# Closing PSUM banks one by one over two rows ahead of a norm, and moving weight splits between engines

## The reference

```
first block, two layers:   hs = hs + rms_norm(mixer(rms_norm(hs)))     mixer: gated delta net, then mLSTM
                           hs = hs + rms_norm(conv_ffn(rms_norm(hs)))
second block, two layers:  x = layer_norm(ALPHA * x + mixer(x))        mixer: conv + window attention, then GLA + MLA
                           x = layer_norm(ALPHA * x + swiglu(x))
```

## Time and profile before

| | |
|---|---|
| three runs | 1445.07, 1447.41, 1447.57 us; median 1447.41 us |
| profiled execution | span 1443.1 us from its first to its last instruction; no other time is given for it. The median lies 4.3 us above the span |
| busy share | PE 99%, PEld 95%, DVE 70%, ACT 54%, POOL 20% |
| mean granted clock of TensorE | 0.999 |
| weight splits | ACT 397 of 1.06 us, DVE 397 of 1.27 us |

### The profile page before, as it was taken

How to read it: one execution, slowest core, us unless ns; L and a number is a source line. 1 busy time by engine, 2 the same in 40 slices (tenths; PEclk the granted TensorE clock), 3 DMA queues, 4 the chain that set the end, 5 groups by cost and what they waited for, 6 DMA issues and landing times.

```text
span 1443.1 us, 31771 instructions
## 1 busy us (share of the span) xinstructions
PE 1423.5 (99%) x11333; PEld 1363.9 (95%) x11333; DVE 1013.4 (70%) x1701; ACT 779.4 (54%) x1399; POOL 294.0 (20%) x348
## 2 busy tenths in 40 slices
PE   9999999999999999999999999999999999999997
PEld 8999888899999999999999999999999989999986
DVE  7884957659876477569888477587664687776645
ACT  6556324556655366466565356464453567654542
POOL 3804002103444000002544000013330012033310
PEclk9999999999999999999999999999999999999999
DMA  7551231244655535344666544546556433565552
GB/s 256 177 175 47 88 101 47 93 142 160 190 175 175 175 119 189 103 146 128 193 189 189 182 134 152 164 146 200 183 168 204 152 116 118 163 217 186 183 180 91
DMA packets 60996, 223.57 MB, mean 155 GB/s; under 512 B 6768, under 2 KB 6896, under 8 KB 60528
## 3 DMA queue, kind: packets, MB, share of 16 engines
q1 hardware_dynamic: 60624, 220.17, 48.1%
q10 hardware_dynamic: 288, 2.23, 0.4%
HBM read 221.32 MB, written 1.05 MB: 154 GB/s over the span
## 4 chain that ended last, share of the span: by engine, by line
PE 81%; DVE 12%; issue 3%; ACT 3%; DVEq 1%; ACTq 0%; POOL 0%; POOLq 0%
PE bank L440 20%; PE bank L441 20%; PE bank L442 20%; DVE wlo L415 3%; PE bank L461 2%; PE bank L1168 2%; PE bank L462 1%; PE bank L468 1%; DVE bank L947 1%; PE bank L3284 1%; PE bank L3285 1%; PE bank L3287 1%; ACT cv L831 1%; DVE cv L839 1%; DVE work L1782 1%
## 5 line engine op out<-in xcount | busy, mean ns | idle before, releaser
L415 DVE TENSOR_TENSOR wlo<-raw,whi 128x1024 fp32r<-128x1024 f32 x397 | 501.4, 1268 | 249.3 <-ACT whi L410 248.8
L410 ACT ACTIVATE whi<-raw 128x1024 fp32r<-128x1024 f32 x397 | 415.1, 1056 | 288.6 <-PE bank L442 240.6
L440 PE MATMUL bank<-xs,whi 128*128 128x258 f32 (+2 forms) x1984 | 569.2, 287 | 0.0
L441 PE MATMUL bank<-xs,whi 128*128 128x258 f32 (+2 forms) x1984 | 563.9, 284 | 0.0
L442 PE MATMUL bank<-xs,wlo 128*128 128x258 f32 (+2 forms) x1984 | 561.6, 283 | 0.0
L440 PEld LDWEIGHTS bank<-xs,whi 128*128 128x128 f32 x1984 | 374.2, 189 | 3.0 <-issue 1.6
L442 PEld LDWEIGHTS bank<-xs,wlo 128*128 128x128 f32 x1984 | 375.0, 189 | 0.0
L441 PEld LDWEIGHTS bank<-xs,whi 128*128 128x128 f32 x1984 | 374.3, 189 | 0.6 <-issue 0.2
L440 PE MATMUL bank<-hf,whi 128*128 (+3 forms) x848 | 241.3, 285 | 2.0 <-DVE cv L839 0.8
L441 PE MATMUL bank<-hf,whi 128*128 (+3 forms) x848 | 240.3, 283 | 0.0
L442 PE MATMUL bank<-hf,wlo 128*128 (+3 forms) x848 | 240.2, 283 | 0.0
(11 more groups left out here) (516 smaller groups left out, 1671.8 us busy)
## 6 DMA issues: line engine op xcount, KB each, us to landing
raw<-stream SPq DMA_DIRECT2D x412, 512.0 KB, 3.7
con<-consts SPq DMA_DIRECT2D x1, 1284.5 KB, 10.5
big<-mla ACTq DMA_DIRECT2D x1, 1152.0 KB, 7.8
hs_sb<-hs SPq DMA_DIRECT2D x2, 544.0 KB, 4.2
work<-last ACTq DMA_DIRECT2D x1, 1024.0 KB, 9.1
y_out<-work SPq DMA_DIRECT2D x4, 256.0 KB, 2.0
par<-params SPq DMA_DIRECT2D x1, 420.0 KB, 7.9
par<-params SPq DMA_DIRECT2D x1, 224.0 KB, 4.8
```

The source lines that it names most:

```text
L410: nc.scalar.activation(whi[:, s, :], raw[:, s, :], ACT.Copy).then_inc(hi_split, 1)
L415: nc.vector.tensor_tensor(wlo[:, s, :], raw[:, s, :], whi[:, s, :].bitcast(F32), ALU.subtract).then_inc(block_split, 1)
L440: nc.tensor.matmul(out_, whi[:, slot, w], hi, start=start, stop=False)
L441: nc.tensor.matmul(out_, whi[:, slot, w], lo, start=False, stop=False)
```

## The change

- `pe_wide`: the last two rows become `last_two`: for each bank the three matmuls of the last row but one and the three of the last. It waits at its start for the last block and for both slices. Banks close six matmuls apart; both blocks count as used at the seventh bank's end.
- RMS seams: DVE adds the squares of banks 0 to 6 (`FIRST_SUM` 7) and copies banks 0 to 5 (`IN_BANK` 6), alternating the two for each bank. PE sums two operands in place of four. The third block's two halves are both made by DVE (`third_split`) behind these; ACT's `split_hi` of it is gone.
- `add_y`: the product for tile m+1 is issued ahead of the addition for tile m, which waited for its own product.
- LayerNorm seams: DVE adds tiles 0 to 6 (`YSUM` 7), PE sums two operands in place of six. The third block's low half is cut in two (`third_low`): one ahead of the mean, one in the wave; PE waits for the second at k = 4.
- The second block's low half is made by POOL (`second_lo`) in all seven seams, behind a wait for the first block's.
- ACT's table load ahead of a seam stands before the splits of the output projection, not behind them.

```diff
+    def second_lo(pool, phase):
+        n = FIRST_BLOCK[phase] + 1
+        s = n % SLOTS
+        pool.wait_ge(block_split, splits(n - 1))
+        pool.wait_ge(hi_split, splits(n))
+        nc.gpsimd.tensor_tensor(wlo[:, s, :], raw[:, s, :], whi[:, s, :].bitcast(F32), ALU.subtract).then_inc(block_split, 1)
...
+        def last_two():
+            pe.wait_ge(block_split, splits(b0 + n - 1))
+            for k in (n - 2, n - 1):
+                ready(pe, k, None)
+            for m in range(8):
+                for k in (n - 2, n - 1):
+                    last = three(rhs_out(g0 + m, phase), (b0 + k) % SLOTS, m, hf[:, half[k], T], hf[:, half[n + k], T], False, k == n - 1)
+                    if m == 7:
+                        last.then_inc(block_used, 1)
+                    elif k == n - 1:
+                        last.then_inc(*S("wide", "pe").mark(f"{phase}_m{m}"))
...
-    FIRST_SUM, IN_BANK = 5, 5
+    FIRST_SUM, IN_BANK = 7, 6
...
-        sums_pe(pe, name, post_src(name), g, ((5, True, False), (6, False, False), (0, False, False), (7, False, True)), T1, POST_FIRST[name])
+        sums_pe(pe, name, post_src(name), g, ((0, True, False), (7, False, True)), T1, POST_FIRST[name])
...
-        split_hi(act, used_after(phase) + AHEAD - 1)
...
+        for m in range(FIRST_SUM):
             dve.wait_ge(*S("norm", "act").at(f"{name}_{m}"))
+            if m:
+                if m > 1:
+                    dve.wait_ge(*v.at(f"{name}_sum{m - 1}"))
+                nc.vector.tensor_tensor(sq[:, 0, lo:T1], sq[:, 0, lo:T1], sq[:, m, lo:T1], ALU.add).then_inc(*v.mark(f"{name}_sum{m}"))
+            if m < IN_BANK:
+                scaled(m)
+        third_split(dve, phase)
...
+    def third_split(dve, phase):
+        n = used_after(phase) + AHEAD - 1
+        s = n % SLOTS
+        dve.wait_ge(hi_split, splits(n - 1))
+        dve.wait_ge(block_split, splits(n - 1))
+        dve.wait_ge(block_loaded[s], 16 * (n // SLOTS + 1))
+        dve.wait_ge(block_used, n - SLOTS + 1)
+        nc.vector.tensor_copy(whi[:, s, :], raw[:, s, :]).then_inc(hi_split, 1)
+        split_lo(dve, n)
...
+    def add_y(dve, name, lo):
+        y_step(dve, name, 0)
+        h_step(dve, name, 0)
+        y_step(dve, name, 1)
+        for m in range(1, KC):
+            if m + 1 < KC:
+                y_step(dve, name, m + 1)
+            h_step(dve, name, m)
+            lo(m - 1)
+        lo(KC - 1)
...
-    YSUM = 3
+    YSUM = 7
...
+    def third_low(dve, name, phase, part):
+        n = FIRST_BLOCK[phase] + AHEAD - 1
+        s, w = n % SLOTS, slice(part * BLOCK // 2, (part + 1) * BLOCK // 2)
+        dve.wait_ge(hi_split, splits(n))
+        dve.wait_ge(block_split, splits(n - 1))
+        nc.vector.tensor_tensor(wlo[:, s, w], raw[:, s, w], whi[:, s, w].bitcast(F32), ALU.subtract
+                                ).then_inc(*((block_split, 1) if part else S("norm", "dve").mark(f"{name}_third")))
...
-            split()
+            third_low(dve, name, phase, 0)
...
+            if phase and m == 2:
+                third_low(dve, name, phase, 1)
...
         gdn_pool(pool)
+        second_lo(pool, "up0")
         ffn_pool(pool, 0, G["up0"])
+        second_lo(pool, "ml_in")
         ml_pool(pool)
...
+        nc.scalar.preload_act_table_set(LN_EXP)
         split_all(act, split_hi, "gdn_out", 1, COUNT["gdn_out"] - 2)
-        nc.scalar.preload_act_table_set(LN_EXP)
         post_act(act, "post0", G["post0"], "gdn_out")
...
-        split_all(dve, split_lo, "gdn_out", 1, COUNT["gdn_out"] - 2)
+        split_all(dve, split_lo, "gdn_out", 1, COUNT["gdn_out"] - 3)
```

More of the change, by code:

```diff
@@ L457, in pe_tiles @@
                     o, s = rhs_out(g0 + j, phase), (b0 + j) % SLOTS
+                    by_half = name.startswith("ln") and j == AHEAD - 1
+                    if k == 0 and by_half:
+                        pe.wait_ge(*S("norm", "dve").at(f"{name}_third"))
+                    if k == (KC // 2 if by_half else 0):
+                        pe.wait_ge(block_split, splits(b0 + j))
                     if k == 0:
-                        pe.wait_ge(block_split, splits(b0 + j))
                         pe.wait_ge(bank_free, g0 + j + 1)
@@ L538, in rows @@
                     bank_ready(pe, (g0 + m) % 8)
-                last = three(rhs_out(g0 + m, phase), (b0 + k) % SLOTS, m, hf[:, half[at] if i is None else at, T], hf[:, half[lo] if i is None else lo, T], k == 0, k == n - 1)
-                if i is None and k == n - 1 and m < 7:
-                    last.then_inc(*S("wide", "pe").mark(f"{phase}_m{m}"))
+                last = three(rhs_out(g0 + m, phase), (b0 + k) % SLOTS, m, hf[:, half[at] if i is None else at, T], hf[:, half[lo] if i is None else lo, T], k == 0, False)
             if done:
                 last.then_inc(block_used, 1)
+        def last_two():
[9 more added lines that the diff above has]
+                        last.then_inc(*S("wide", "pe").mark(f"{phase}_m{m}"))
         if n == 22:
@@ L549, in pe_wide @@
                     rows(k, i)
-            for k in range(17, 22):
+            for k in range(17, n - 2):
                 rows(k)
+            last_two()
         else:
@@ L558, in pe_wide @@
                         between(pe, k)
-            for k in range(together, n):
+            for k in range(together, n - 2):
                 rows(k)
+            last_two()
     def pe_sum(pe, name, g, src, T):
@@ L706, in post_act, with post_dve, y_step @@
         nc.scalar.activation(rs[:, 1, lo:T1], rs[:, 1, lo:T1], ACT.Exp, scale=-0.5).then_inc(*S("norm", "act").mark(f"{name}_scale"))
-    def post_dve(dve, name, g, row, split):
+    def post_dve(dve, name, g, row, phase):
         v, lo = S("norm", "dve"), POST_FIRST[name]
         def scaled(m):
+            nc.vector.tensor_scalar(y[:, m, lo:T1], bank[(g - 8 + m) % 8][:, lo:T1], pv("norm_w", row * KC + m), None, ALU.mult).then_inc(bank_free, 1)
+        for m in range(FIRST_SUM):
             dve.wait_ge(*S("norm", "act").at(f"{name}_{m}"))
[L713 to L722, removed]
-        split()
+            if m:
[5 more added lines that the diff above has]
+        third_split(dve, phase)
         banked[name] = g, row
         dve.wait_ge(*S("norm", "act").at(f"{name}_scale"))
-    def add_y(dve, name, m):
+    def third_split(dve, phase):
[7 more added lines that the diff above has]
+        split_lo(dve, n)
+    def y_step(dve, name, m):
         v, t = S("norm", "dve"), slice(POST_FIRST[name], T1)
@@ L777, in lo @@
                                            ALU.mult, ALU.subtract).then_inc(*S("norm", "dve").mark(f"{name}_lo{m}"))
[L779 to L783, removed]
+        add_y(dve, post, lo)
         split_lo(dve, fourth(phase))
@@ L793, in next_act @@
         t = slice(PRE_FIRST[name], T1)
+        act.wait_ge(hi_split, splits(fourth(phase) - 1))
         split_hi(act, fourth(phase))
@@ L821, in last_act @@
             if m == 4:
+                act.wait_ge(hi_split, splits(fourth("ev_in") - 1))
                 split_hi(act, fourth("ev_in"))
@@ L2341, in ln_act, with ln_dve @@
         act_scale(act, name + "v", g + 1, rs[:, 0, 0:T2], T2, D, eps_ln, meanwhile=lambda: split_hi(act, fifth(phase)) if phase == "od_in" else None)
-    def ln_dve(dve, n, which, layer, phase, wide, split):
+    def third_low(dve, name, phase, part):
[5 more added lines that the diff above has]
+                                ).then_inc(*((block_split, 1) if part else S("norm", "dve").mark(f"{name}_third")))
+    def ln_dve(dve, n, which, layer, phase, wide):
         name, g = f"ln{n}", G[f"lm{n}"]
@@ L3087, in odd_pool @@
         pool.wait_ge(block_used, used_after("down2"))
+        pool.wait_ge(block_split, splits(FIRST_BLOCK["od_in"] + 1))
         for h in range(4):
@@ L3367, in _ @@
         gdn_pool(pool)
+        second_lo(pool, "up0")
         ffn_pool(pool, 0, G["up0"])
+        second_lo(pool, "ml_in")
         ml_pool(pool)
+        second_lo(pool, "up1")
         ffn_pool(pool, 1, G["up1"])
+        second_lo(pool, "ev_in")
+        second_lo(pool, "up2")
         ffn_pool(pool, 2, G["up2"])
+        second_lo(pool, "od_in")
         odd_pool(pool)
+        second_lo(pool, "up3")
         ffn_pool(pool, 3, G["up3"])
@@ L3442, in _ @@
         gdn_mix_dve(dve)
-        split_all(dve, split_lo, "gdn_out", 1, COUNT["gdn_out"] - 2)
-        post_dve(dve, "post0", G["post0"], 1, lambda: split_lo(dve, used_after("gdn_out") + AHEAD - 1))
+        split_all(dve, split_lo, "gdn_out", 1, COUNT["gdn_out"] - 3)
+        post_dve(dve, "post0", G["post0"], 1, "gdn_out")
         next_dve(dve, "post0", "pre1", 2, "up0")
         ffn_dve(dve, 0, G["up0"])
-        split_all(dve, split_lo, "down0", 1, COUNT["down0"] - 2)
-        post_dve(dve, "post1", G["post1"], 3, lambda: split_lo(dve, used_after("down0") + AHEAD - 1))
+        split_all(dve, split_lo, "down0", 1, COUNT["down0"] - 3)
+        post_dve(dve, "post1", G["post1"], 3, "down0")
         next_dve(dve, "post1", "pre2", 4, "ml_in")
```

(8 more changed lines are left out.)

34 lines of the change are left out of this document (18 added, 16 removed).

## The result

The changed kernel takes 1453.38 us (median of four runs, 1450.9 to 1454.77) against 1446.26 for the kernel before (four runs): ratio 1.0049, 95% interval 1.0037 to 1.006, 7.1 us slower. Forecast were 1451.0 and a range of 1441 to 1456. The profiled execution, the slowest of the four, has a span of 1452.6.

The account below looks back on a forecast made before the run. PE held 81% of the chain, DVE set the seams' wave pace. Seam terms 0.15 + 0.15 + 0.38 + 0.61 + 2.31 = +3.6 on 1447.4 gave 1451.0 us, range 1441 to 1456.

Parts of the forecast that it names:

- The hold: At all seven seams, DVE's first sum of two SBUF tiles waits for POOL's subtraction, 1.53 us late; chance 0.62.
- nothing was made good behind it: At `post0`, DVE's 0.77 us of work per bank against closings 0.75 apart recovers none of the 1.53 us delay.
- The first product: First product after the sums comes later: +0.93 us at `post0`, +1.09 at `post3`; first centred tile at `ln0` +0.77.
- DVE isn't held: Rival: DVE's sums pass POOL, each of seven first products 1.53 us earlier, 1440.3 us in all; chance 0.13.
- in part: Rival: POOL starts later or shorter, or DVE catches up; some 0.5 us less per seam, 1445 to 1448; chance 0.15.
- The forecast of 10.97: At `post0`, from first product to next block with PE bounding the wave: 10.97 us, 0.78 less than before.
- The edits at nothing: Table load, `last_two`'s wait, third block's copy and low half, and queue and wait changes: costed at 0 us.
- where DVE has slack: In the LayerNorm seams, half of `third_low` moves into the wave, where DVE was taken to have time: 0 us.
- the sum: All seven seams' changes added together: +3.6 us, of which the three LayerNorm seams are +2.31.
- a case of its own: Rival: PE's wait at the seams lowers the clock, 2 us in each, 1453 up to 1465; chance 0.10.
- the sixteen slow matmuls: Behind PE's wait at a seam, the first sixteen matmuls at 0.25 instead of 0.125: 2 us, seven times 14.

Follow-up runs that it names:

- e1: Changed kernel with the second block's low half back on DVE in all seven seams; 1449.29 us, ratio 1.0021 to the kernel before.
- e2: Changed kernel with DVE's order altered so copies from banks (LayerNorm seams: four `y`) precede the first sum, beside POOL's subtraction; 1447.26 us.
- e3: Changed kernel with POOL's subtraction in four pieces of 256 columns; 1442.26 us, ratio 0.9982 to the kernel before.
- e6: Kernel before the change with only the second block's low half moved to POOL in all seven seams; 1445.15 us, ratio 0.9994.
- e5: Kernel before the change with only `add_y`: the product for tile m+1 ahead of the addition for tile m; 1442.32 us, ratio 0.9976.
- e9: As e7, but at `ln1` both halves of the third block's low half ahead of the mean; 1438.8 us, ratio 0.9959 to the kernel before.
- e4: Changed kernel with 16 (LayerNorm seams: 20) unread matmuls ahead of PE's sums to keep the clock up; 1451.32 us, ratio 1.0037.
- e7: As e3, but DVE adds six banks or tiles in place of seven and PE sums three operands; 1439.01 us, ratio 0.9952.
- e8: As e3, but POOL's subtraction in eight pieces of 128 columns; 1447.62 us, ratio 1.0005 to the kernel before.

## Why the prediction was right, and where it was mis-sized

**The hold**, the likeliest case, is what happened, and e1, e2, e3 and e6 show it from four sides. POOL's subtraction took 2.40 (2.38 forecast) and began where it was put; sum 1 took 2.03 (about 1.9), PE waited 1.92 (nearly 2); nothing was made good behind it, as steps of 0.76 met closings of 0.75. The first product came 1.08 later at `post0` (0.93 forecast), 1.13 at `post3` (1.09), 0.90 to 0.93 at the LayerNorm seams (0.77). The rivals that DVE isn't held, or in part, are out. The Trainium skill, "SBUF — State Buffer", section "Who interferes with whom", says that a DVE instruction with two SBUF inputs contends with a GpSimd instruction that reads SBUF, that one with at most one SBUF input, outside DVE's two-port modes, doesn't, and that the ports the two share are an exclusive lock. The traces agree: e2's copies at 0.50 and its sum at 0.86, and e3, where the turns change with each piece.

**`add_y`** gave 0.71 at `post0` (0.78) and 0.50 at `post3` (0.48); e5 gets 2.5 by it alone. The forecast of 10.97 from product to next block was 11.04.

**The edits at nothing** were at nothing, all but one. `third_split`'s copy took 0.68 (0.65), and its low half ended 0.46 ahead of the first product. The table load in `ml_out` stayed hidden: from the end of the wave at `post1` to the end of `ml_out` it is 113.75 after and 113.87 before. The exception is the second half of `third_low` "in the wave, where DVE has slack": at `ln1` DVE has none, because the pair sums stand in that wave. It cost 0.42 there, and e9 takes just that away. At `ln0` and `ln2` it cost 0.1.

**The size.** Forecast +3.6, measured +7.1, of which the seams of the trace show 6.8. With the clock at 1.00 (e4) the seams are 5.1 above before (100.9 less 95.8): 1.5 more than the sum, of which 0.6 is that half of the low half and the rest the first products, 0.04 to 0.2 later each than worked out. The other 1.7 is the clock. I had held it for a case of its own, with a chance of 0.10 and 2 us in each seam; it is a part of the held case, falls in some seams and not in others, and cost 0.2 to 1.1 where it fell. No row stood behind the sixteen slow matmuls of that price; what the runs show is a fall of 3.41 us. So the forecast was right in its mechanism, its sign and its range, and too small by three terms: the half of the low half that I put at nothing, the first products, and a fall of the clock that belongs to the wait that I had forecast myself. That 1453.38 is only 2.4 off 1451.0, where the change itself was missed by 3.5, is luck: the forecast stood on 1447.4 for the kernel before, and its median of four runs is 1446.26.

## What to carry to other kernels

An instruction moved to GpSimd has its price not where it runs but in what VectorE does beside it: list VectorE's instructions with two SBUF inputs in that stretch, and count the rest of GpSimd's instruction for the first of them. Where they must overlap, a GpSimd instruction in a few pieces lets the other engine in between (four pieces here took 11 us off, eight only 6, as the sums met the eighths at a worse point), or VectorE's work from PSUM is put beside it. Try each part of a change by itself: here one was worth 3 us alone (`add_y`) and one cost nothing alone (GpSimd's part). The third, the merged rows with seven sums, wasn't run alone; it lost both with GpSimd's part (7 us) and without it (4 us, e1), with GpSimd's work in four pieces the whole came to the time of `add_y` alone (1442.26 in e3, 1442.32 in e5), and only with six sums below it (1439.01, e7).

## What the runs showed of the hardware

A sum of two SBUF tiles that starts beside GpSimd's subtraction is held until some 0.12 before GpSimd's recorded end, with pieces of 1024, 256 and 128 columns alike: with 1.72 left it loses 1.61 (changed kernel, `post0`), with 0.56 it loses 0.44 (e2), with 0.40 it loses 0.28 (e8), with 0.27 it loses 0.15 (e3).

At the seams the clock's falls follow waits of PE of about two microseconds, but not each of them: of ten waits of 1.90 to 2.41 ahead of the sums (seven in the changed kernel, three in e1) five were followed by a stretch at 0.50, the shortest being one of 1.90; of 25 waits there of 0.74 to 1.66 (e1, e2, e3, e8) none. The longer wait isn't the more likely one: 2.41 at `ln1` kept its clock, 1.90 at `post1` lost it. One execution of each kernel was profiled, so which seam has a fall may differ in another. Before, no wait of that length had stood in a wave.
